# Output projection token-major: y loaded and W_out streamed, the residual kept by tokens; cross scores of the second four heads moved into the next product

## The reference

```python
u = rmsnorm(h, g_mix);  z = u @ w_in            # 8 HGRN2 heads (128), then 4 GLA heads (dk 128, dv 256)
o = chunked_gated_recurrence(q, k, v, log_a)    # per head
y = concat(head_rmsnorm(o) * silu(gate))        # (512, 2048)
h = x + y @ w_out                               # output projection
m = rmsnorm(h, g_mlp) @ w_up
h = h + square(relu(m)) @ w_down
h = h + sigmoid(rmsnorm(h, g_ple) @ w_pg) * (p @ w_pp)
return rmsnorm(h, g_final)
```

## Time and profile before

| | us |
|---|---|
| median of 3 runs | 2561.64 (2557.96 to 2562.38) |
| profiled execution, its own time | 2562.51 |
| its span, first to last instruction | 2560.8 |
| PE busy | 2497.7 |
| DVE busy | 1666.4 |
| ACT busy | 1004.1 |
| POOL busy | 258.9 |

### The profile page before, as it was taken

One profiled execution on the slowest core, in us unless ns is written; L12 is line 12 of the kernel. 1 busy time (PEld: TensorE's weight loads), 2 busy tenths in 40 slices (PEclk: granted clock), 3 DMA queues, 4 the chain that ended last, 5 costly groups with the idle time before them and its releaser, 6 DMA issues.

```text
span 2560.8 us, 29814 instructions
## 1 busy us (share of the span) xinstructions
PE 2497.7 (98%) x11408; PEld 2060.1 (80%) x11408; DVE 1666.4 (65%) x1998; ACT 1004.1 (39%) x1350; POOL 258.9 (10%) x199
## 2 busy tenths in 40 slices
PE   7999999999999999999999999999999999999996
PEld 6888888888777788888888888888888888888884
DVE  6766666678777424434444444459998898895466
ACT  5444444443444213333333333234333333345354
POOL 5111111112114333000000000000000000000111
PEclk9999999999999999999999999999999999999998
DMA  7232232332333233655555555567456656543323
GB/s 232 67 82 80 68 82 66 82 83 66 82 81 116 82 98 88 206 178 185 177 180 182 184 182 176 178 229 268 175 173 229 232 206 221 190 154 119 111 91 115
DMA packets 417003, 371.14 MB, mean 145 GB/s; under 512 B 5452, under 2 KB 352232, under 8 KB 416776
## 3 DMA queue, kind: packets, MB, share of 16 engines
q1 hardware_dynamic: 416808, 369.77, 45.5%
q10 hardware_dynamic: 96, 0.02, 0.0%
HBM read 302.66 MB, written 67.11 MB: 144 GB/s over the span
## 4 chain that ended last, share of the span: by engine, by line
PE 64%; DVE 3%; ACT 1%; issue 0%; POOL 0%; DVEq 0%; POOLq 0%; ACTq 0%
PE bank L1844 21%; PE bank L1846 21%; PE bank L1845 21%; DVE u_lo L1567 0%; PE bank L2104 0%; PE bank L2060 0%; DVE h L1748 0%; DVE w_lo L1719 0%; ACT w_hi L763 0%; DVE gate_e L1741 0%; DVE gate_e L1739 0%; DVE w_lo L1195 0%; ACT w_hi L1085 0%; DVE gate_e L1745 0%; DVE gate_e L1731 0%
## 5 line engine op out<-in xcount | busy, mean ns | idle before, releaser
L1844 PE MATMUL bank<-u_hi,w_hi 128*128 128x512 f32 x2176 | 864.4, 397 | 17.5 <-DVE w_lo L1195 6.1
L1846 PE MATMUL bank<-u_hi,w_lo 128*128 128x512 f32 x2176 | 849.4, 390 | 0.0
L1845 PE MATMUL bank<-u_lo,w_hi 128*128 128x512 f32 x2176 | 848.9, 390 | 0.0
L1844 PEld LDWEIGHTS bank<-u_hi,w_hi 128*128 128x128 f32 x2176 | 409.8, 188 | 110.0 <-issue 16.9
L1845 PEld LDWEIGHTS bank<-u_lo,w_hi 128*128 128x128 f32 x2176 | 409.8, 188 | 86.7 <-issue 4.1
L1846 PEld LDWEIGHTS bank<-u_hi,w_lo 128*128 128x128 f32 x2176 | 409.4, 188 | 86.2
L1195 DVE TENSOR_TENSOR w_lo<-w_raw,w_hi 128x2048 fp32r<-128x2048 f32 x132 | 306.8, 2325 | 201.8 <-ACT w_hi L763 201.8
L1844 PE MATMUL bank<-w_hi,forms 128*128 128x512 f32 x896 | 349.5, 390 | 0.4 <-DVE h L1662 0.4
L1846 PE MATMUL bank<-w_hi,forms 128*128 128x512 f32 x896 | 348.8, 389 | 0.0
L1845 PE MATMUL bank<-w_lo,forms 128*128 128x512 f32 x896 | 348.7, 389 | 0.0
L763 ACT ACTIVATE w_hi<-w_raw 128x2048 fp32r<-128x2048 f32 x137 | 260.5, 1904 | 215.3 <-PE bank L1846 201.7
(11 more groups left out here) (243 smaller groups left out, 2662.4 us busy)
## 6 DMA issues: line engine op xcount, KB each, us to landing
w_raw<-in_w_up SPq DMA_DIRECT2D x64, 1024.0 KB, 6.4
w_raw<-in_w_in SPq DMA_DIRECT2D x57, 1024.0 KB, 5.6
forms_scratch<-stage SPq DMA_DIRECT2D x32, 1792.0 KB, 7.3
forms<-forms_scratch SPq DMA_DIRECT2D x56, 1024.0 KB, 7.2
ring<-in_w_down SPq DMA_DIRECT2D x40, 1024.0 KB, 5.6
w_raw<-in_w_down SPq DMA_DIRECT2D x24, 1024.0 KB, 5.3
ring<-in_w_pg SPq DMA_DIRECT2D x20, 1024.0 KB, 5.1
w_raw<-in_w_out SPq DMA_DIRECT2D x16, 1024.0 KB, 5.8
```

The lines of the kernel that those rows point to most:

```text
L1844: pe.matmul(ps, whi, xhi, start=start, stop=False, skip_group_check=shared)
L1845: pe.matmul(ps, whi, xlo, start=False, stop=False, skip_group_check=shared)
L1846: return pe.matmul(ps, wlo, xhi, start=False, stop=stop, skip_group_check=shared)
```

## The change

- **Start.** No copy of transposed x, no scratch in DRAM. ACT and DVE read the PSUM bank themselves.
- **GLA passes.** ACT's w_hi of the next first unit goes between levels 5 and 6, DVE's w_lo before `cross_products`. PE does the four cross scores inside the next product, ahead of its fourth tile.
- **Output projection.** For column block q (512 channels) and quad i (4 tiles of y), a unit of W_out is 4 x 512 wide. The y tile (128 channels x 128 tokens) is loaded, W_out streams, four banks hold the four token blocks. DVE adds each to h, which is now x by tokens, loaded directly from the input. In the last column the finished h is turned on PE into the channel form that the up-projection needs (12 tiles there, 4 inside the first product of the up-projection), and split by ACT and DVE out of PSUM.
- **Row scale.** The sum of squares is taken by ACT from h (`square_mix`). The scale of the up-projection's norm is no longer applied before relu: its square multiplies the results of the down-projection, in the addition to h. ACT does relu out of PSUM, then the square. POOL's sums and PE's sum over partitions go.

```diff
-            for c in range(KT // 4):
-                sp.wait_ge(xT_copied, 4 * c + 4)
-                sp.dma_start(xT_dram[4 * c:4 * c + 4].rearrange("k q s -> q k s"), h[:, 4 * c:4 * c + 4, :])\
-                    .then_inc(xT_stored[c], 16)
...
+            for t in range(NT):
+                sp.dma_start(h[:, :, t * P:(t + 1) * P], x_tok[:, t, :].rearrange("q (k c) -> q k c", c=P)).then_inc(h_landed, 16)
+                if t % 2:
+                    load_out(3 + t // 2)
...
-                level_exps(hd, range(EARLY + 1, LEVELS))
-                cross_exps(hd)
+                level_exps(hd, range(EARLY + 1, LEVELS - 1))
                 if hd.gla:
                     slot(5)
+                level_exps(hd, range(LEVELS - 1, LEVELS))
+                cross_exps(hd)
...
-            split_y_read(range(6))
+            split_y_read(range(2))
+            out_hi(1)
+            split_y_read(range(2, 6))
             place_cross(last)
             place_values(last)
             silu(last, "gate", 0)
             split_y_read(range(6, 10))
             silu(last, "gate", 1)
+            out_hi(2)
             split_y_read(range(10, KT - 2))
             square_o(last)
-            split_hi(Unit(U_OUT + 1), U_OUT)
             head_norm(last)
+            out_hi(3)
...
+            for n in range(3, KT):
+                out_hi(n + 1)
+                if n % OUT_QUADS == 0:
+                    for t in range(NT):
+                        square_mix(n // OUT_QUADS - 1, t)
+                if n > 12:
+                    for k in range(4 * (n - 13), 4 * (n - 12)):
+                        turn_out_hi(k)
...
             def square_up(i):
-                act.wait_ge(z_evac, U_MLP + i + 1)
+                act.wait_ge(z_done, U_MLP + i + 1)
...
-                act.activation(araw[:, i % 4, :], relu[:, i % 2, :], ACT.Square).then_inc(a_ready, 1)
+                act.activation(araw[:, i % 4, :], bank[Unit(U_MLP + i).slot][:, :], ACT.Relu).then_inc(z_evac, 1)
+                act.wait_ge(z_evac, U_OUT + i + 1)
+                act.activation(araw[:, i % 4, :], araw[:, i % 4, :], ACT.Square).then_inc(a_ready, 1)
...
-                v.wait_ge(xT_ps, k + 1)
-                v.tensor_copy(h[:, k, :], bank[2 + k % 6][:, :]).then_inc(xT_copied, 1)
...
-                    v.tensor_tensor(dst, dst, by_tile(bank[bk + t][:, :]), op).then_inc(added, 1)
+                    rs = rs_mlp[:, sign, 2 * rows + t:2 * rows + t + 1]
+                    v.scalar_tensor_tensor(out=dst, in0=by_tile(bank[bk + t][:, :]), scalar=rs, in1=dst, op0=ALU.mult,
+                                           op1=ALU.add).then_inc(added, 1)
...
+            output_gate(last, {0: lambda: out_lo(1)})
+            out_lo(2)
             split_y(range(POOL_Y, KT - 2))
-            split_lo(Unit(U_OUT + 1))
             head_mean(last)
             head_output(last)
+            out_lo(3)
             split_y(range(KT - 2, KT))
...
+            for t in range(NT):
+                turn_out_lo(8 + t)
+                add_out(NT - 1, t)
+            for k in range(12, KT):
+                turn_out_lo(k)
...
             def iteration(hd, prev):
-                product(hd.unit(0), hd.unit(0).u, hd.unit(0).slot, {4: lambda: values(prev)})
+                between = {4: lambda: values(prev)}
+                if prev.gla:
+                    between[3] = lambda: cross_scores(prev)
+                product(hd.unit(0), hd.unit(0).u, hd.unit(0).slot, between)
...
+            def out_step(q, i, t, k):
+                at = k * S
+                slot = Unit(U_OUT + OUT_QUADS * q + i).slot
+                rows, y_at = slice(t * P, (t + 1) * P), 4 * i + k
+                return tri(bank[OUT_BANKS[q % 2][t]][:, :], u_hi[:, y_at, rows], u_lo[:, y_at, rows],
+                           w_hi[:, slot, at:at + S], w_lo[:, slot, at:at + S], y_at == 0, y_at == KT - 1)
+
+            def first_quad():
+                pe.wait_ge(w_lo_ready, U_OUT + 1)
+                pe.wait_ge(z_evac, U_OUT)
+                for k in range(4):
+                    y_ready_tile(k)
+                    for t in (0, 1):
+                        out_step(0, 0, t, k)
+                    if k == 0:
+                        cross_scores(last)
+                    if k == 2:
+                        values(last)
+                pe.wait_ge(level_placed, LEVELS * HEADS)
+                pe.wait_ge(cross_placed, HEADS)
+                for k in range(4):
+                    if k == 1:
+                        outputs(last)
+                    for t in (2, 3):
+                        last_mm = out_step(0, 0, t, k)
+                last_mm.then_inc(z_done, 1)
...
+                        if i == 1 and k == 3:
+                            last_mm.then_inc(z_done, 1)
+                            square_sums(last)
...
+            def turn_out(k):
+                pe.wait_ge(out_added, NT * (k // 4 + 1) if k >= 12 else NT * (NT - 1))
+                if 2 <= k < 14:
+                    pe.wait_ge(u_lo_ready, KT + POOL_Y + k - 1)
+                for t in range(NT):
+                    last_mm = pe.transpose(turn_bank(k)[:, t * P:(t + 1) * P], h_tile(k, t), ident[:, :])
+                last_mm.then_inc(h_turned, 1)
...
+            def mix_tile(k):
                 def run():
+                    if k == 4:
+                        turn_out(12)
+                        turn_out(13)
+                    if k == 6:
+                        turn_out(14)
+                        turn_out(15)
                     pe.wait_ge(u_lo_ready, KT + POOL_Y + k + 1)
```

More of the change, by code:

```diff
@@ L288, in build @@
         x_landed = [sem(f"x_landed{c}") for c in range(NT)]
-        xT_stored = [sem(f"xT_stored{c}") for c in range(4)]
-        h_landed = [sem(f"h_landed{c}") for c in range(KT // 4)]
+        h_landed = sem("h_landed")
         out_stored = sem("out_stored")
@@ L1568, in split_h, with turn_out_lo @@
+            def turn_out_lo(k):
+                v.wait_ge(u_hi_ready, 2 * KT + k + 1)
+                v.scalar_tensor_tensor(out=u_lo[:, k, :], in0=turn_bank(k)[:, :], scalar=vec1[:, V_MLP + k:V_MLP + k + 1],
                                        in1=u_hi[:, k, :].bitcast(F32), op0=ALU.mult, op1=ALU.subtract)\
                     .then_inc(u_lo_ready, 1)
-            for k in range(KT):
-                if k == KT - 1:
-                    add_to_h(R_MLP - 1, (R_MLP - 1) % 2, k)
-                split_h(k, V_MLP, 2)
@@ L1577, in relu_up @@
-            def relu_up(i):
-                unit = Unit(U_MLP + i)
-                v.wait_ge(z_done, unit.u + 1)
-                if i >= 2:
-                    v.wait_ge(a_ready, i - 1)
-                v.scalar_tensor_tensor(out=relu[:, i % 2, :], in0=bank[unit.slot][:, :], scalar=0.0,
-                                       in1=rs_u[:], op0=ALU.max, op1=ALU.mult).then_inc(z_evac, 1)
+            for n in range(3, KT):
+                if n % OUT_QUADS == 0:
+                    for t in range(NT):
+                        add_out(n // OUT_QUADS - 1, t)
+                out_lo(n + 1)
+                if 12 < n < KT - 1:
+                    for k in range(4 * (n - 13), 4 * (n - 12)):
+                        turn_out_lo(k)
@@ L2034, in y_tile @@
-                return run
-            others, own = range(KT - 2), range(KT - 2, KT)
-            first, second = (Unit(U_OUT), U_OUT, U_OUT % 2), (Unit(U_OUT + 1), U_OUT + 1, (U_OUT + 1) % 2)
-            product(*first, {k: y_tile(k) for k in others}, others)
-            product(*second, (), others)
-            product(*first, {k: y_tile(k) for k in own}, own)
-            product(*second, (), own)
-            with pe.Fori(1, KT // 2) as i:
-                for j in range(2):
-                    unit = Unit(U_OUT + j, 2, i)
-                    product(unit, unit.u, unit.slot, read=u_read if j else None)
@@ L2067, in _ @@
                 if i == 0:
-                    between = {k: h_tile(k) for k in range(KT)}
-                elif 4 <= i < 4 + KT:
-                    between = {KT // 2: turn_h(i - 4)}
-                product(unit, unit.u, unit.slot, between, read=x_read if i == UPS - 1 else None)
+                    between = {k: mix_tile(k) for k in range(KT)}
+                product(unit, U_OUT + i, unit.slot, between, read=x_read if i == UPS - 1 else None)
             def down_half(G, l):
```

287 lines of the change are left out of this document (139 added, 148 removed).

## The result

The changed kernel takes 2544.5 us (median of 4 runs, 2544.1 to 2545.9) where the kernel before took 2560.8 in the same measurement (2558.0 to 2562.4). The ratio is 0.9941, with a 95% interval of 0.9928 to 0.9953: 16.3 us faster, a small change but clear of its interval, and 2.5 us above the forecast time of 2542. The profiled execution took 2545.92 us against the 2562.5 of before, 16.6 less, where the sum said 19.8. That difference of about 3 us is what the rest of this document is about.

The account below looks back on a forecast made before the run. Work on PE (TensorE) was taken to set the time, so only its gaps could be won: 1.8 + 4.0 + 11.8 + 2.3 - 0.15 = 19.8 off 2562.5, less 0.9, gives 2541.8, forecast 2542 us, range 2537 to 2546.

Parts of the forecast that it names:

- PE's own work: Output projection: 768 matmuls either way at 0.2265 us with operands swapped; range 0 to +6 us, taken 0.
- The rival of a dearer swap: Output projection: swapped operands cost as in the gate stage, 5.9 us more, 2548; chance 0.06.
- The start: First x tiles: without DVE's copy, PE goes on about 26.1 instead of 27.94; 1.8 us won (0.5 to 2.2).
- The passes: Ends of the GLA passes: new order of splits and cross scores shortens PE's gaps; 4.0 us won, range 0 to 5.
- Into the output projection: Last GLA head to output projection: one gap of 2.9 us instead of 16.4 lost; 11.8 us won.
- split to 812.5, cross_products to 813.95, evacuation to 814.6: DVE's order before the output projection, letting PE idle only 811.83 to 814.7, 2.9 us.
- rival (f): Down-projection: additions cost DVE as much as its operations beside POOL, 1.65 us; 157 us slower, 2699; chance 0.02.
- one lower-clock spell, charged 1.7 us: Behind the 2.9 us gap before the output projection: 8 matmuls at 0.43 us; may be 0 in some runs.
- Rival (a): Output projection: fourth split and y tiles 14, 15 late, clock falls again; 11.8 becomes 7, 2547; chance 0.14.
- Into the up-projection and the up-projection: PE's wait of 1.21 for POOL's sum over squares and two passes of 1.12 go: 2.3 us won; up-projection itself 0.
- The down-projection: 224 additions gain a per-partition scalar, 0.751 against 0.679 us each; DVE's free time covers nearly all: -0.15 us.
- Rival (c): Down-projection: DVE's dense order fills up and additions wait on drains, +4 us, 2546; chance 0.05.

Follow-up runs that it names:

- copy_back: The changed kernel with DVE again copying each x tile from PSUM into h, and ScalarE and DVE reading the copy: 2547.6 us.
- after_again: The changed kernel run once more without any edit, as base for the other variants: 2544.9 us.
- pool_waits: The changed kernel, but POOL may not begin its u_lo of y before the last head's cross_products are done: 2542.6 us.
- undo_gla_order: The changed kernel with the old order (cross scores in late scores, next weights' split behind cross_products and cross_exps) in all four GLA heads: 2545.0 us.
- tile0_on_dve: The changed kernel with last evacuation before cross_products in each GLA head; at the last, DVE forms u_lo of tile 0, POOL waits for cross_products: 2538.3 us.
- last_like_before: The changed kernel with the old order (cross scores in late scores, weight split behind cross_products) at the last GLA head alone: 2541.0 us.
- adds_plus_256: The changed kernel with one more unread 128x256 DVE addition behind each of the down-projection's 224 additions: 2580.4 us, one run.
- evac_first: The changed kernel with DVE's last evacuation (unit 5) ahead of cross_products in each GLA head: 2542.2 us.

## Why the prediction was right or wrong

**PE's own work: right.** The matmuls start 0.226 us apart with W_out moving (0.2265 forecast). In 846 to 966 us PE's three groups hold 177 each, 531 in 120 us, without a gap. The rival of a dearer swap is out.

**The start: the mechanism was right, the size too small.** 1.8 was forecast, 2.4 came by the two first traces, and copy_back lost 2.8 of it again (2.0 when each is held against the kernel before on its chip). The prediction let PE wait 0.4 us for u_lo of tile 6 (25.73 to 26.1); it never waited for it. The other 0.2 to 0.6 is not traced to a step. Of the gain, 1.7 us went into the spell at 78 us in the profiled execution. That is no cost of the change: after_again and five of its siblings do not have it.

**The passes: right, a little more than forecast.** 5.1 for 4.0. Pass 0 to 1 gave 0.95 (0.7 forecast), the other two 2.07 each (1.65). The gaps are 0.85 and 0.86 (0.8 forecast). Set inside a product, the four cross scores cost 1.1 instead of 1.55 us.

**Into the output projection: wrong, and this is the miss.** The step that failed is the chain "split to 812.5, cross_products to 813.95, evacuation to 814.6". In the same paragraph POOL was put at work from 812.4, so DVE and POOL were to run side by side, and cross_products was priced at 1.45, its time with POOL idle. They took 4.65. The row with the right price was in use further down: 1.64 us for an operation beside POOL (the same line takes 0.69 at 831.80, with POOL idle) was the price of rival (f), a case to which I gave 0.02, and I did not apply it where the overlap was certain. The 5.98 - 2.9 = 3.1 us of it are the whole of the 14.1 - 11.0 missing here. pool_waits, undo_gla_order and tile0_on_dve each take the overlap away in another manner: PE waits 2.4, 3.4 and 4.6 us less than in after_again, and gets from the late scores to the norm sums 1.7, 3.3 and 4.4 us sooner.

The rest of that paragraph held: one lower-clock spell, charged 1.7 us, which cost 1.6 (40.0 less 5.98 of waiting, against the 32.4 without it in last_like_before); no wait for the second, third and fourth split, none for tiles 14 and 15. Rival (a) did not come, though it had only 1 us of cover.

**Into the up-projection and the up-projection: right.** PE goes from the last product through a turn into the next product without a wait; the sum over squares and its two passes are gone. ScalarE's ReLU takes 0.598 (0.59 assumed), and PE is busy 698.0 of 698 us. PE's timeline, against the earlier trace rows:

```profile
1001.57 0.60 PE L2089 MATMUL bank<-ident,h 128*128 128x128 f32 x4
1001.92 0.47 PE L1833 MATMUL bank<-u_hi,w_hi 128*128 128x512 f32 x1
```

**The down-projection: right.** 0.744 us an addition (0.751 assumed), one wait, 0.55 against the 0.43 of the earlier trace rows:

```profile
1711.75 0.47 PE L1833 MATMUL bank<-w_hi,forms 128*128 128x512 f32 x1 [0.55 <-DVE h L1667]
```

adds_plus_256 shows that its cover was worked out rightly too. The prediction set the trace against the Trainium skill ("VectorE: DVE Perf Modes", The DRAIN you can't avoid) as if it let no operation start before the former has drained. The same paragraph of the Trainium skill goes on that a next operation that is not held starts earlier. The trace agrees with that: behind an operation of 0.42 us the next starts after 0.33.

**What was not on the list.** None of the rivals said that the exit's own chain would stretch. Rival (c), 2546, came nearest in size and (a), 2547, next, both for reasons that did not occur. That the changed GLA order, taken as a whole, was worth only about 2 us was not seen either: its passes were forecast at 4.0, its cost at the exit at nothing.

**How near it came, and luck.** On the profiled execution the sum was 19.8 and the trace shows 16.7. The exit gave 3.1 less and the spell at 78 us took 1.7; the passes gave 1.1 more and the start 0.6. That forecast and median lie only 2.5 us apart is in part luck: errors of both signs met.

## What to carry to other kernels

When a change lets a second engine start earlier, write down what the first one does in that time and price both as they run together: a price taken from a trace in which they ran one after the other does not hold. Look for it on small operations at a stage's exit, where three or four of 0.3 to 0.6 us stand between an engine that waits and its next product. And follow an order that helps inside a loop to the loop's last round: what stands behind it there is other work, and here it took back 3.3 of the 5.1 us that the three rounds before had won; the last round can have an order of its own (last_like_before, tile0_on_dve).

## What the runs showed of the hardware

- **DVE beside POOL.** Operations of DVE with both inputs in SBUF that started behind a POOL operation ended only 0.15 to 0.3 us after it: 0.28 became 1.36, and 0.42 became 1.49, about the 1.3 to 1.7 us of one POOL operation, whatever their own size. The 128x384 that began together with POOL's first kept its 0.55, and POOL's took 1.68. The evacuation with one input in PSUM kept its 0.68. The Trainium skill says so in "SBUF — State Buffer" (Who interferes with whom): a DVE instruction with two SBUF inputs contends with a GpSimd instruction that reads SBUF, and the later one waits for the whole of the other. The trace agrees in both directions: in the kernel before, where DVE's split of 2.29 us had started first, POOL's first u_lo took 2.85 instead of 1.27.
- **Spells of lower clock are not a property of the kernel alone.** The same code had them at different places in two profiles (78 us in one, 15 to 25 in the other). Runs of last_like_before lie 4 us apart in two lots; that this is the clock too is likely, but the slower lot left no trace. A gap of 2.04 had the lower level behind it in evac_first, and one of 2.30 in the kernel before and one of 2.37 in last_like_before had not. The Trainium skill says in "TensorE: Matmul & The Clock Gate" (Part 1) that the clock gate's monitor runs free and does not start anew with the kernel; these profiles agree with it.
- **DVE's operations overlap by 0.09 us** in the down-projection even where DVE is full: behind one of 0.42 us the next starts after 0.33.
